# RWKV-7 recurrence on one core: key and value products kept with the two heads exchanged, and issued in pairs with others on the four 64x64 quarters of TensorE

## The reference, cut to what matters

```python
def step(S, inp):
    r_t, w_t, k_t, v_t, kk_t, b_t = inp
    sa = jnp.einsum('bhvk,bhk->bhv', S, -kk_t)
    S = S * w_t[:, :, None, :] + sa[..., None] * b_t[:, :, None, :] + v_t[..., None] * k_t[:, :, None, :]
    return S, jnp.einsum('bhvk,bhk->bhv', S, r_t)
```

## Time and profile before

| | |
|---|---|
| median of 3 runs | 3404.09 us |
| profiled execution | 3405.31 us |
| its span | 3403.5 us, 81781 instructions |
| busy over the span | PE 87%, DVE 39%, ACT 33%, POOL 4% |
| recurrence | 880 to 1696 us of the span |
| one turn of the recurrence, at full clock | 49.66 us |
| granted TensorE clock, mean | 0.95 |
| DMA over the span | 85 GB/s mean, 44 GB/s in the recurrence |

### The profile page before, as it was taken

The page is one execution under the profiler, slowest core; times in us unless marked ns, Lnnn a source line. Parts: engine busy times, 40 slices in busy tenths (PEclk is TensorE's granted clock), DMA queues, the critical chain, the costliest instruction groups (busy, mean ns, idle before and its releaser), DMA issues. The chain is left out here.

```text
span 3403.5 us, 81781 instructions
## 1 busy us (share of the span) xinstructions
PE 2977.2 (87%) x37120; PEld 2774.3 (82%) x37120; DVE 1322.4 (39%) x2139; ACT 1126.1 (33%) x1557; POOL 130.4 (4%) x123
## 2 busy tenths in 40 slices
PE   5999999999688888888759938999999999994993
PEld 4999999999577777777659817999999999993993
DVE  4343333311365566656421153343333343333113
ACT  5344333322234434333321223333333333332111
POOL 0000000000000000000000010000000000000001
PEclk8999999999799999999979969999999999996997
DMA  2323333332111111111132162222222232223223
GB/s 109 107 101 111 110 111 112 112 118 88 53 35 51 43 42 44 44 50 35 32 127 88 46 211 104 78 92 93 74 99 80 85 102 80 85 77 113 74 84 95
DMA packets 91233, 288.79 MB, mean 85 GB/s; under 512 B 18720, under 2 KB 25248, under 8 KB 70432
## 3 DMA queue, kind: packets, MB, share of 16 engines
q1 hardware_dynamic: 79136, 257.19, 22.3%
q10 hardware_dynamic: 9216, 17.83, 1.4%
q0 software_dynamic: 2560, 8.91, 0.8%
HBM read 229.56 MB, written 54.34 MB: 83 GB/s over the span
## 5 line engine op out<-in xcount | busy, mean ns | idle before, releaser
L1204 PE MATMUL e_pair<-e_x_hi,e_w_hi 128*128 128x272 f32 x2048 | 455.6, 304 | 57.2 <-DVE e_w_lo L1467 57.2
L123 PE MATMUL ab_pair<-ab_x_hi,ab_w_hi 128*128 128x272 f32 x2048 | 433.1, 293 | 24.0 <-ACT ab_x_hi L292 19.2
L1204 PE MATMUL e_pair<-e_x_hi,e_w_lo 128*128 128x272 f32 x2048 | 428.5, 291 | 0.0
L1204 PE MATMUL e_pair<-e_x_lo,e_w_hi 128*128 128x272 f32 x2048 | 427.5, 291 | 0.0
L123 PE MATMUL ab_pair<-ab_x_hi,ab_w_lo 128*128 128x272 f32 x2048 | 425.7, 289 | 0.0
L123 PE MATMUL ab_pair<-ab_x_lo,ab_w_hi 128*128 128x272 f32 x2048 | 424.4, 289 | 0.0
L1204 PEld LDWEIGHTS e_pair<-e_x_hi,e_w_hi 128*128 128x128 f32 x2048 | 323.4, 191 | 90.2 <-issue 82.9
L123 PEld LDWEIGHTS ab_pair<-ab_x_hi,ab_w_hi 128*128 128x128 f32 x2048 | 325.8, 189 | 29.8 <-issue 21.0
L335 DVE TENSOR_TENSOR ab_w_lo<-ab_raw,ab_w_hi 128x2048 fp32r<-128x2048 f32 x64 | 146.6, 2293 | 523.6 <-ACT ab_w_hi L267 523.6
L1204 PEld LDWEIGHTS e_pair<-e_x_lo,e_w_hi 128*128 128x128 f32 x2048 | 326.0, 191 | 0.0
L1204 PEld LDWEIGHTS e_pair<-e_x_hi,e_w_lo 128*128 128x128 f32 x2048 | 325.1, 192 | 0.0
(11 more groups left out here) (305 smaller groups left out, 4468.1 us busy)
## 6 DMA issues: line engine op xcount, KB each, us to landing
ab_raw<-in_w_in SPq DMA_DIRECT2D x64, 1024.0 KB, 4.7
e_raw<-in_hgrn_in SPq DMA_DIRECT2D x64, 1024.0 KB, 4.8
o_raw<-in_rwkv_wo SPq DMA_DIRECT2D x16, 1024.0 KB, 4.8
o_raw<-in_hgrn_wo SPq DMA_DIRECT2D x16, 1024.0 KB, 4.8
o_y<-scr_yz SPq DMA_DIRECT2D x32, 272.0 KB, 3.0
e_Ss<-in_hgrn_s SPq DMA_DIRECT2D x16, 512.0 KB, 4.8
out_hgrn_s<-e_Sd SPq DMA_DIRECT2D x16, 512.0 KB, 7.1
ab_nxt<-in_x SPq DMA_DIRECT2D x4, 1088.0 KB, 9.0
```

Of the source, the lines that this page charges most:

```text
L123: mm = pe.matmul(out[:, a, 0:TH], w, x[:, kt, a * TH:(a + 1) * TH], start=(kt == 0 and n == 0), stop=(kt == KT - 1 and n == 2))
L1204: mm = pe.matmul(out[:, a, 0:TH], w, x[:, kt, a * TH:(a + 1) * TH], start=(kt == 0 and i == 0), stop=(kt == KT - 1 and i == 2))
```

## The change

Two products are issued together, quarter by quarter: one that stays in its half (the diagonal quarters), and one whose output (or input) half is exchanged, which takes the two other quarters. Each goes to its own PSUM bank; there is a new bank `f_ps`. For this Ktok, Vtok, Mak and Mrk are kept with the two heads exchanged. `by_token` is gone.

- `mab` and `mak` become one group `strict` (L767 is its place); it waits in addition for `y_ev`, ACT's copy of the outputs of the tile before out of `y_ps`.
- `btok` and `ktok` become `bk`, and it stands before `level_yt(j, 1)`, where `btok` stood behind it.
- `mrb` and `mrk` become `incl`, at the place of `mrb`; DVE masks Mrb and Mrk one after the other ahead of `add_tit(j, 2)`.
- `atok` and `vtok` become `av`, at the place of `ktok`, in level 3. Nothing stands between x and yt in level 4 any more, only an `iterate` in level 5.
- Back: R0 and TA together; U0 together with the Ktok Vtok half of Wh (into `f_ps`), ahead of `lora_a` instead of behind it; G together with the Vtok Mrk products of all chunks (into `y_ps`, left open for accumulation). Wh has 16 matmuls left instead of 32, each chunk of the chain one stacked product less.
- ACT and DVE keep all their instructions; their waits follow the new groups.

```diff
+            def quarter(out, o_half, lhsT, rhs, i_half, start=True, stop=True):
+                return pe.matmul(out[rows(o_half)], lhsT[rows(i_half)], rhs[rows(i_half)], start=start, stop=stop,
+                                 skip_group_check=not (start and stop))
+
-            def by_token(out, src):
+            def channel_pair(same, l_same, r_same, swapped, l_swap, r_swap):
                 for c in range(NCH):
-                    mm = stacked(cut(out, c), cut(src, c), k.eye)
+                    for hh in range(2):
+                        quarter(cut(same, c), hh, cut(l_same, c), r_same if r_same is k.eye else cut(r_same, c), hh)
+                        mm = quarter(cut(swapped, c), 1 - hh, cut(l_swap, c),
+                                     r_swap if r_swap is k.eye else cut(r_swap, c), hh)
+                return mm
+
+            def token_pair(same, l_same, r_same, c0, swapped, l_swap, r_swap, keep_open):
+                for c in range(NCH):
+                    for hh in range(2):
+                        mm = quarter(cut(swapped, c), hh, cut(l_swap, c), cut(r_swap, c), 1 - hh,
+                                     c == 0 or not keep_open, not keep_open)
+                        if c >= c0:
+                            mm = quarter(cut(same, c), hh, cut(l_same, c), cut(r_same, c), hh)
                 return mm
...
+                    pe.wait_ge(s.atok, i + 1)
                     pe.wait_ge(s.tit, (NL - 1) * (i + 1))
-                    chunks(b0, Mak, Vtok).then_inc(s.r0_mm, 1)
+                    token_pair(b1, TiT, Atok, 1, b0, Mak, Vtok, False).then_inc(s.r0ta_mm, 1)
...
                 if back:
-                    pe.wait_ge(s.atok, i + 1)
-                    chunks(b1, TiT, Atok, 1).then_inc(s.ta_mm, 1)
+                    pe.wait_ge(s.r0, i + 1)
+                    pe.wait_ge(s.ktok, i + 1)
+                    token_pair(b0, TiT, R0, 0, f_ps, Ktok, Vtok, True).then_inc(s.u0_mm, 1)
                 if front:
                     pe.wait_ge(s.sgw, j + 1)
                     over_halves(w2[:, 1, :], lora[1]).then_inc(s.lora_a, 1)
                 if back:
-                    pe.wait_ge(s.r0, i + 1)
-                    chunks(b0, TiT, R0).then_inc(s.u0_mm, 1)
                     pe.wait_ge(s.ta, i + 1)
                     pe.wait_ge(s.btok, i + 1)
-                    chunks(b1, TA, Btok, 1).then_inc(s.g_mm, 1)
+                    pe.wait_ge(s.mrk, i + 1)
+                    token_pair(b1, TA, Btok, 1, y_ps, Vtok, Mrk, True).then_inc(s.g_mm, 1)
                     pe.wait_ge(s.u0, i + 1)
-                    pe.wait_ge(s.ktok, i + 1)
                     for c in range(NCH):
-                        stacked(cut(b0, c), cut(Ktok, c), cut(Vtok, c), True, False)
-                        mm = stacked(cut(b0, c), cut(Btok, c), cut(U0, c), False, True)
+                        mm = stacked(cut(f_ps, c), cut(Btok, c), cut(U0, c), False, True)
...
-                        stacked(cut(y_ps, c), cut(Vtok, c), cut(Mrk, c), True, False)
                         mm = stacked(cut(y_ps, c), cut(U0, c), cut(Mrb, c), False, c == 0)
...
+                if back:
+                    pe.wait_ge(s.y_ev, i + 1)
                 if front:
                     pe.wait_ge(s.at, j + 1)
                     pe.wait_ge(s.bt, j + 1)
+                    pe.wait_ge(s.kt, j + 1)
                     if back:
                         pe.wait_ge(s.state, NCH * (i + 1))
-                    chunks(b0, bt, at).then_inc(s.mab_mm, 1)
+                    channel_pair(b0, bt, at, y_ps, kt, at).then_inc(s.strict_mm, 1)
...
                 if front:
-                    pe.wait_ge(s.kt, j + 1)
-                    chunks(y_ps, kt, at).then_inc(s.mak_mm, 1)
                     pe.wait_ge(s.MT, j + 1)
                     level_x(j, 1)
...
+                    pe.wait_ge(s.mak, j + 1)
+                    channel_pair(y_ps, bt, k.eye, f_ps, kt, k.eye).then_inc(s.bk_mm, 1)
                     level_yt(j, 1)
-                    pe.wait_ge(s.mak, j + 1)
-                    by_token(y_ps, bt).then_inc(s.btok_mm, 1)
                     level_x(j, 2)
...
-                    chunks(y_ps, bt, rho).then_inc(s.mrb_mm, 1)
+                    pe.wait_ge(s.ktok, j + 1)
+                    channel_pair(y_ps, bt, rho, f_ps, kt, rho).then_inc(s.incl_mm, 1)
                     level_yt(j, 2)
...
                     level_x(j, 3)
                     pe.wait_ge(s.mrb, j + 1)
-                    by_token(y_ps, kt).then_inc(s.ktok_mm, 1)
+                    pe.wait_ge(s.mrk, j + 1)
+                    channel_pair(y_ps, at, k.eye, f_ps, vt, k.eye).then_inc(s.av_mm, 1)
                     level_yt(j, 3)
                     iterate(j, 0)
                     level_x(j, 4)
-                    pe.wait_ge(s.ktok, j + 1)
-                    chunks(y_ps, kt, rho).then_inc(s.mrk_mm, 1)
                     level_yt(j, 4)
                     iterate(j, 1)
                     level_x(j, 5)
-                    pe.wait_ge(s.mrk, j + 1)
-                    by_token(y_ps, at).then_inc(s.atok_mm, 1)
                     iterate(j, 2)
                     level_yt(j, 5)
-                    pe.wait_ge(s.atok, j + 1)
-                    by_token(y_ps, vt).then_inc(s.vtok_mm, 1)
...
-                    dve.wait_ge(s.mrb_mm, j + 1)
+                    dve.wait_ge(s.incl_mm, j + 1)
                     dve.tensor_tensor(by_chunk(Mrb), by_chunk(y_ps), each(k.incl), ALU.mult).then_inc(s.mrb, 1)
+                    dve.tensor_tensor(by_chunk(Mrk), by_chunk(f_ps), each(k.incl), ALU.mult).then_inc(s.mrk, 1)
                     add_tit(j, 2)
```

More of the change, by code:

```diff
@@ L593, in rwkv_recurrence @@
         q = ps("q", [P, 2, 512])
-        b0, b1, y_ps, m_ps = (ps(n, [P, 512]) for n in ("b0", "b1", "y", "m"))
+        b0, b1, y_ps, f_ps, m_ps = (ps(n, [P, 512]) for n in ("b0", "b1", "y", "f", "m"))
         s = R.sems("const_in r_in k_in v_in z_in w2_in S0_in zeroed "
@@ L597, in rwkv_recurrence @@
                    "at bt kt at_b bds kds "
-                   "r0_mm r0 ta_mm ta u0_mm u0 g_mm g wh_mm rhoe_mm rhoe chain_mm state y_mm y_ev eyed "
-                   "mab_mm MT tit0 ti x_mm X yt_mm tit "
-                   "mak_mm mak mrb_mm mrb mrk_mm mrk btok_mm btok ktok_mm ktok atok_mm atok vtok_mm vtok "
+                   "r0ta_mm r0 ta u0_mm u0 g_mm g wh_mm rhoe_mm rhoe chain_mm state y_mm y_ev eyed "
+                   "strict_mm MT tit0 ti x_mm X yt_mm tit mak "
+                   "incl_mm mrb mrk bk_mm btok ktok av_mm atok vtok "
                    "sm_mm sMs stoks sR_mm sR sMU_mm sU sy_mm sy Vm Um Sd sd_mm snew "
@@ L657, in _ @@
                     if j + 1 < KT:
-                        sp.wait_ge(s.vtok_mm, j + 1)
+                        sp.wait_ge(s.av_mm, j + 1)
                         sp.wait_ge(s.bv, j + 1)
@@ L742, in _ @@
                     chunks(b1, TA, Mrb, 1).then_inc(s.rhoe_mm, 1)
-                    pe.wait_ge(s.mrk, i + 1)
                 for c in range(NCH):
@@ L780, in _ @@
                     pe.wait_ge(s.kds, j + 1)
+                    pe.wait_ge(s.rho, j + 1)
                     pe.wait_ge(s.v_in, 16 * (j + 1))
@@ L856, in _ @@
                 if back:
-                    act.wait_ge(s.r0_mm, i + 1)
+                    act.wait_ge(s.r0ta_mm, i + 1)
                     act.copy(R0[:, :], b0[:, :]).then_inc(s.r0, 1)
@@ L862, in _ @@
                 if back:
-                    act.wait_ge(s.ta_mm, i + 1)
+                    act.wait_ge(s.r0ta_mm, i + 1)
                     act.copy(TA[:, C:], b1[:, C:]).then_inc(s.ta, 1)
@@ L894, in _ @@
                     act.copy(toks[:, :], m_ps[:, 4 * C:7 * C]).then_inc(s.stoks, 1)
-                    act.wait_ge(s.btok_mm, j + 1)
+                    act.wait_ge(s.bk_mm, j + 1)
                     act.copy(Btok[:, :], y_ps[:, :]).then_inc(s.btok, 1)
+                    act.copy(Ktok[:, :], f_ps[:, :]).then_inc(s.ktok, 1)
                 if back:
@@ L905, in _ @@
                     act.copy(Rs[:, :], cut(m_ps, 0)).then_inc(s.sR, 1)
-                    act.wait_ge(s.ktok_mm, j + 1)
-                    act.copy(Ktok[:, :], y_ps[:, :]).then_inc(s.ktok, 1)
-                    act.wait_ge(s.atok_mm, j + 1)
+                    act.wait_ge(s.av_mm, j + 1)
                     act.copy(Atok[:, :], y_ps[:, :]).then_inc(s.atok, 1)
-                    act.wait_ge(s.vtok_mm, j + 1)
-                    act.copy(Vtok[:, :], y_ps[:, :]).then_inc(s.vtok, 1)
+                    act.copy(Vtok[:, :], f_ps[:, :]).then_inc(s.vtok, 1)
                     act.wait_ge(s.sy_mm, j + 1)
@@ L985, in _ @@
                         dve.wait_ge(s.wp_out, 16 * i)
-                    dve.tensor_tensor(by_chunk(S), by_chunk(b0), We[i % 2][:, 0:NCH].unsqueeze(2).broadcast_to([P, NCH, HD]),
+                    dve.tensor_tensor(by_chunk(S), by_chunk(f_ps), We[i % 2][:, 0:NCH].unsqueeze(2).broadcast_to([P, NCH, HD]),
                                       ALU.mult).then_inc(s.state, 1)
```

(6 more changed lines are left out.)

2 lines of the change are left out of this document (removed).

## The result

The changed kernel takes 3444.3 us (median of 4 runs, 3434.4 to 3452.5) against 3404.0 (3403.4 to 3404.4) for the kernel before on the same chip: a ratio of 1.0112 [1.0092, 1.0132], 40 us slower. The prediction was 3423 with a range to 3442. The sign came as forecast, and so did its cause, falls of the clock in nearly every turn; their place and length, and with them the size, did not.

A forecast was written before the change was run, and what follows sets the result against it. A PE-DVE loop inside the levels was taken to set the pace. Terms of -1.10 us over 15 turns gave -16.5; clock falls, 16 x 2.2, added 35.2: +18.7 in all, forecast 3423 us, range 3386 to 3442.

The forecast's parts named there:

- Term 1: At strict, the new wait for ACT's copy of the outputs starts it later: +0.34 us a turn.
- Term 2: bk ahead of yt1 takes 0.96 us with nothing to hide it: +0.81 us a turn.
- Term 3: At incl, DVE masks both Mrb and Mrk ahead of the addition: +0.30 us a turn.
- Terms 4 and 5: Levels 3 to 5: products in DVE's time save only 0.09 us; vtok gone behind level 5 saves 0.94 us.
- Term 6: In the back, U0 copied sooner and a shorter Wh bring RhoE earlier: -1.40 us a turn.
- Term 7: In the DVE-paced chain of chunks, one product less per chunk counts once: -0.12 us a turn.
- The clock: Low clock from level 4 or 5 until the dense part behind level 5, in nearly every turn: 2.2 us each.
- The bound of 3.5 us for a fall: Upper price per turn, if a second fall in the chain or a longer low-clock stay adds to it.
- The rival that the clock holds: In the recurrence no added falls, so the full-clock sum stands: 3388 us; chance 0.18.
- The rival that the quarters don't overlap: Strict, bk, incl, av and G cost 0.93 us more each, 4.6 a turn: 3457 us; chance 0.10.

The follow-up runs named there:

- experiment 2: Changed kernel plus eight useless stacked identity products in each of levels 4 and 5: 3394.8 us, 0.9956 of the kernel before.
- experiment 5: experiment 2 with the pair bk moved behind yt1: 3375.0 us, 0.9912 of the kernel before.
- experiment 6: experiment 5 with Mak in f_ps, strict without its wait for y_ev, and Mrk masked behind level 2's transposition: 3363.4 us, 0.9875 of the kernel before.
- experiment 7: Changed kernel plus eight useless stacked identity products in level 4 alone: 3421.6 us, 1.0046 of the kernel before.
- experiment 8: Changed kernel plus eight useless stacked identity products behind yt5, where vtok stood, none in levels 4 and 5: 3431.1 us, 1.0075 of the kernel before.
- experiment 4: Changed kernel with each pair's first group issued whole, then the second, same operands and banks: 3505.6 us, 1.0289 of the kernel before.
- experiment 1: Kernel before without products mrk in level 4 and atok in level 5, Mrk and Atok holding zeros: 3430.5 us, 1.0070 of the kernel before.
- experiment 3: Changed kernel with strict, incl and back paired, but btok, ktok, atok, vtok single; Mak in f_ps, Mrk masked later: 3359.7 us, 0.9867 of the kernel before.

## Why the prediction was wrong in size

Three distances make up a turn: from the masking of Mab to x5, from x5 to DVE's update of the samples' state, and from there to the next masking. From the timelines (before, for the turn of the earlier trace rows that begins at 1146.22; experiment 2 at full clock; the changed kernel), in us:

| stretch | before | experiment 2 | difference | predicted | changed kernel |
|---|---|---|---|---|---|
| masking to x5 | 21.91 | 22.94 | +1.03 | +0.81 + 0.30 = +1.11 | 22.94 |
| x5 to samples' state | 7.47 | 6.54 | -0.93 | -0.09 - 0.94 = -1.03 | 9.51 |
| samples' state to masking | 20.28 | 18.82 | -1.46 | +0.34 - 1.40 - 0.12 = -1.18 | 18.82 |
| turn | 49.66 | 48.30 | -1.36 | -1.10 | 51.27 |

The operations that end the middle stretch stand here as the timeline of DVE has them, in the kernel before
```profile
1175.60 0.69 DVE L1096 TENSOR_TENSOR c_Sd<-c_m,c_Sd 128x512 f32<-128x512 f32 x1 [3.60 <-PE c_m L678]
```
in experiment 2 (x5 starts at 1168.32)
```profile
1174.86 0.69 DVE L1108 TENSOR_TENSOR c_Sd<-c_m,c_Sd 128x512 f32<-128x512 f32 x1 [2.67 <-PE c_m L678]
```
and in the changed kernel (x5 at 1178.69)
```profile
1188.20 0.69 DVE L1102 TENSOR_TENSOR c_Sd<-c_m,c_Sd 128x512 f32<-128x512 f32 x1 [5.06 <-PE c_m L678]
```

- **Term 1, strict's wait: right.** Experiments 5 and 6 differ by 0.34 us between the back's state and the masking (10.08 and 9.74).
- **Term 2, bk ahead of yt1: right,** +0.74 instead of +0.81. yt1 starts at 1160.66, 2.70 us behind x1 (1157.96), where 2.75 was said.
- **Term 3, two maskings ahead of the addition: right.** In the changed kernel they start at 1166.74 and 1167.35 and the addition at 1167.95, 1.21 us behind the first as against 0.94 in the earlier trace rows; with bk's share taken away experiments 5 and 6 leave 0.30.
- **Terms 4 and 5, gaps free and vtok paid: right.** yt5 starts 1.94 us behind x5 in the changed kernel where it was 2.03, the 0.09 of the prediction. The filler behind x5 takes that away again in experiment 2 (2.03), so its middle stretch is shorter by 0.93; in experiment 7's turns at full clock, without that filler, it is 6.50, shorter by 0.97. Experiment 8 pays 0.94 for a group where vtok stood. Levels 3 and 4 of the changed kernel are still 4.63 us each, as in the earlier trace rows.
- **Term 6, the back: right.** From the samples' state to the back's state it is 8.73 instead of 10.15 us: -1.42, predicted -1.40.
- **Term 7, the chain: too small,** -0.38 instead of -0.12 (from the back's state to the masking 10.09 us instead of 10.13, with the +0.34 of term 1 in it). The larger part is not the product that is gone: DVE's rk takes 0.78 us (1198.71) instead of 1.08, as POOL's product c_Sd, which ran beside it, now starts only at 1199.10, 2.17 us behind the back's state instead of 1.23. It then runs beside kkn, which takes 1.37 instead of 0.77 us, but there DVE had waited 0.64 us for PE's link behind the bonus product in any case. POOL waits in both kernels for ACT's exponential c_We, which ends at 1186.90 before and 1199.02 after. Against the samples' state that is 0.48 us earlier (10.82 behind it instead of 11.30), while DVE's work gained the 1.42 of term 6 and so ran ahead of POOL.
- **The clock: the mechanism right, its price mis-sized.** This is the failed step. The prediction priced a turn's fall at 2.2 us, as two products of the loop at +0.77 and 0.7 for the samples. It measures 4.13 (52.43 - 48.30), of it 2.97 in the common turn, and all of those 2.97 lie between x5 and the samples' state (9.51 - 6.54). Two things were off. First the place: the fall was thought to begin in levels 4 and 5 and to slow x and yt there, but in the common turn it begins at yt5 and covers the samples' dense products. yt5 pays 0.63 us (from its start to the next product 1.56 instead of 0.93 in experiment 2), and from there to the state update it is 6.01 instead of 3.58: 2.4 us, not 0.7. x5 is at full clock in such a turn. Only in five of the six longer turns does the fall reach the loop itself, from x5 on in three and from level 4 on in two. Second the length: the low clock holds for 136.5 us in 14 turns, 9.75 a turn. The three falls of the kernel before lasted 3.4 us each, the one in the earlier trace rows at 1239.3 among them; the changed kernel has stretches of 6.8 us in the common turn and of 10.2 to 17.1 in the turns of 53.0 to 54.5, of which three have another of 3.4 at 8.0 us behind the masking.

The bound of 3.5 us for a fall came from the same idea of where it lies and so failed with it. The row to read was there: at the low clock a product's pitch is 1.73 instead of 0.96 us, which in a stretch where PE never waits is nearly half a microsecond lost for each at the low clock. The prediction itself had said that what would upset the sum most was a longer stay.

The 36.1 us taken apart: 14 x 4.13 = 57.8 for the clock, 14 x 1.36 = 19.0 gained by the packing, and 2.7 that the kernel before lost to falls of its own (14 x (49.85 - 49.66)) give 57.8 - 19.0 - 2.7 = 36.1, the difference of the 14 turns. The first two shares both rest on the 48.30 us of a turn at full clock; that they add up is no test of it. The prediction had 35.2 and 16.5 for the first two.

What the low clock costs by place, from turns with and without it: 0.18 to 0.24 us for each microsecond at the end of a turn (experiment 2: 48.90 - 48.30, experiment 5: 48.38 - 47.56, for 3.4 each), 0.23 to 0.29 in the three turns of the kernel before, 0.28 from level 4's yt to yt5 (experiment 8: 1.90 for 6.8), 0.44 from yt5 on (2.97 for 6.8) and 0.46 in level 2 (experiment 2, its turns of 50.33 and 50.67: from DVE's addition of level 1 to that of level 2 it is 7.68 and 7.71 us instead of 6.12, for 3.4). The rest of those two turns' surplus lies ahead of that, where PE pauses for 0.24 and 0.56 us inside yt1 without a wait for another engine. The Trainium skill, TensorE: Matmul & The Clock Gate, Terms, puts the penalty at the throttled time times one minus the ratio of the clocks, one half; by that 136.5 us would cost 68, and the trace has 57.8. As a mean it is near, 0.42 for each microsecond where the page has 0.50, but it does not say that the place moves it from 0.18 to 0.46.

The rival that the clock holds came true in no turn of the changed kernel, only once the levels were filled. The rival that the quarters don't overlap fell with experiment 4. The Trainium skill, TensorE: Matmul & The Clock Gate, Part 3, has weight loads overlap running matmuls only where the row group differs. Half of the neighbours in a pair share their rows, the first two by the lines of experiment 4 (1165.51 and 1165.52) among them, which start 0.01 us apart and last 0.27. The pair still takes 0.98 us against 1.5 to 1.7 in sequence, so here the measurement decides against that rule as a bound. The prediction set down that each product has a bank of its own. That does not keep the two row halves of a product apart: in both kernels both write the product's one bank.

**Open.** What sets the length of a low stretch. It was 3.4 us in experiment 1 and 6.8 to 17.1 in the changed kernel, though by the records PE was busy for 3.40 of 3.40 us in the one and for 6.52 of 6.80 in the common turn of the other. The products differ: vtok stood in experiment 1 where the changed kernel has the samples' narrow ones. But with such products put back at that place (experiment 8) it was still 6.8 us. That stays open, and so does why a few falls are left in experiments 2 and 5 (five and three of 14 turns) and none in 3 and 6. It is not known either why six of the 14 turns fall harder than the others; the changed kernel's runs scatter by 18 us, the kernel's before by 1 us on that chip.

## What to carry to other kernels

Before taking work off an engine, ask whether each piece stands on the path or in a gap: here the packing as a whole gave 1.36 us a turn at full clock, and the pieces that it took out of the gaps had given no time but had held the clock up. Pack where the engine is the bound and leave the rest as filler; that version (experiment 3) is 1.3% faster than the kernel before, where packing everything is 1.1% slower. When a fall of the clock is expected, price it where it will lie, and by the dense work behind the gap as much as by the gap itself.

## What the runs showed of the hardware

- Less work can be slower by more than the work was worth: two groups of products left out cost 23 us (experiment 1), and useless ones put in gave 49 to 53 (experiment 2). Products of the identity, mostly zeros, hold the clock as well.
- Pairs of products in all four 64x64 quarters run at once, 64 records in 0.98 us, although quarters share rows, share output partitions in two banks, and each bank is written from both row halves.
- With a product in the gaps of levels 4 and 5 the falls that begin there are gone (experiments 2, 3, 5 and 6). In experiments 3 and 6 the clock then falls in none of the 14 turns of the profiled run, though PE is busy only 563.8 of 698 us in experiment 3; experiments 2 and 5 keep single falls of 3.4 us at a turn's end or, in experiment 2, in level 2.
- An operation of DVE took 1.37 instead of 0.77 us where POOL worked beside it (kkn in the changed kernel), and 1.08 instead of 0.78 (rk in the kernel before); POOL's own product took 1.28 and 1.04 us.
- The same low clock costs 0.18 to 0.29 us for each microsecond where PE has slack and 0.44 to 0.46 where it is the bound.
